# A two-layer encoder trunk on one core: VectorE takes branch B's finished block behind the split of the fourth chunk, where it stood in front of it

## The chip, the cores and the metric

The kernel runs on one core of a Trainium2 chip. The metric is the device time of one execution in microseconds. Three executions of the kernel before gave a median of 2657.65 us (2656.19 to 2660.18).

## The reference

The model is a trunk of two layers over 256 tokens with 2048 channels, all in float32.

```python
for l in range(DEPTH):                                  # 2
    h = rmsnorm(x, norm_mix[l])
    qa, ka, va, qi, ki, wi, qb, kb, vb = split(h @ w_in[l])
    o_a = dsa_branch(qa, ka, va, qi, ki, wi, bias_a)    # 8 heads x 128, top-64 keys
    o_b = swa_branch(qb, kb, vb, sinks[l], bias_b)      # 16 heads x 64, window of 128
    g_a, g_b = split(sigmoid(h @ w_gate[l]))
    merged = g_a * (o_a @ w_branch_a[l]) + g_b * (o_b @ w_branch_b[l])
    x = x + merged @ w_out[l]
    h = rmsnorm(x, norm_mlp[l])
    x = x + square(relu(h @ w_up[l])) @ w_down[l]
return rmsnorm(x, final_norm)
```

The change lies where `g_b * (o_b @ w_branch_b)` is finished and `merged` is formed.

## The kernel before, in words

**Chunks.** All weights stream from HBM once, in chunks of 256 rows by 512 columns (512 KB). A chunk takes four steps. SyncE issues its load into one of four `raw` buffers as soon as the chunk four places ahead of it has been split (`load_unit`, L336). ScalarE copies it, rounded, into `w_hi` (L934). VectorE forms the remainder `w_lo = raw - w_hi` (L1362). TensorE multiplies: for each of 2 row blocks and 2 token halves the three products hi·hi, hi·lo and lo·hi (L590 to L592), 12 matmuls of 512 columns. ScalarE may fill `w_hi` of a chunk once TensorE has finished the chunk four places before it, so the splits run up to four chunks ahead of TensorE.

**Wide chunks.** In some units the odd chunks 1, 3, 5 and 7 are wide: two by two blocks are multiplied with seven products where eight are usual (`seven_products`, L558 to L560, 21 matmuls of 256 columns). For these VectorE first forms sums of the chunk's blocks in `raw` (`weight_sums`, three subtractions and additions, L1371, L1375, L1377). ScalarE's copy has two pieces, the first (L941) straight from the load, the second (L943) from those sums, and VectorE's split covers seven quarters (`split_wide`, L1383). VectorE forms the sums of chunk c+1 before it splits chunk c.

**Branch B.** `C_MIXB` is the first chunk of branch B's part of a layer. For each of four column blocks n of 512 it has a gate unit of 8 chunks (four of them wide), `h @ w_gate`, and a branch unit of 4 plain chunks, `o_b @ w_branch_b`. Below, the chunks of block n are counted 0 to 7 (gate) and 8 to 11 (branch).

What happens with a block:
- When TensorE has finished the gate, ScalarE saves one quarter of the side products (`gate_side`, L1198). That stands in its order in the branch unit in front of chunk 11's copy.
- VectorE adds the side products together behind the split of chunk 11 (`add_up_sides`, L1781 to L1789).
- ScalarE applies tanh (`gate_tanh`, L1203) behind chunk 0's copy of the next gate unit. It is the sigmoid in disguise.
- VectorE takes the block in the next gate unit, at chunk 3 (`take_branch_b`, L1728). It waits for TensorE's end of the branch unit and for the tanh, multiplies gate and branch (L1732, twice), adds branch A's part (L1736), and transposes the sum in 32 by 32 blocks into `spread` (`spread_block`, L1440, twice).
- GpSimd stores `spread` to HBM (L465, 512 KB) and, when the store has landed, reads it back in another order into `moved` with four reads of 128 KB (L470, `pass_on`).
- ScalarE copies `moved`, rounded, into the operand of the output projection (`hi_moved`, L1001). In its order that stands behind chunk 8's copy, in front of chunks 9, 10, `gate_side` and 11. VectorE forms the remainder behind its split of chunk 8 (`lo_moved`, L1464).

The first gate unit of the part takes branch A's last block at the same place (`take_branch_a(3)`, L1720, two instructions, no transposes and no store). Branch B's last block is taken in the first unit of the output projection, whose chunks are all plain.

**Order.** Every engine's order is written out by hand. `unit` (L1386) walks the chunks of a unit: the sums for c+1, then `take` if c is 3, then `at[c]`, then the split of chunk c, then `then[c]`.

Of the kernel before, what the change touches and what calls it, by code (L numbers as in the profile page):

```python
# [114 lines left out]
def trunk_kernel(nc, x, w_misc, w_main, gains, sinks, rel_bias, onehot, final_gain, bias_rows, out):  # L115
    with ExitStack() as ctx:
# [1238 lines left out]
        def _(dve):  # L1355
# [30 lines left out]
            def unit(cl, chunks, take=None, turns=None, taken=None, jobs=None, width=NB, phase=0, first=0, sums=None,  # L1386
                     wide=(), steps=None, at=(), then=()):
                for c in range(first, chunks):
                    if c + 1 in wide:
                        weight_sums(cl, c + 1, steps(wide.index(c + 1)))  # L1390
                    if c == 3 and take:
                        take()
                    if c in at:
                        at[c]()
                    if c in wide:
                        split_wide(cl, c)
                    else:
                        split(cl, c, width, phase)
                    if c in then:
                        then[c]()  # L1400
                    if turns and c in (5, 7):
                        turns((c - 5) // 2)
                    if taken and c == 6:
                        taken()
                    if sums and c == 7:
                        sums()
                    if jobs:
                        jobs(c)

            def unit_done(cl_end):  # L1410
                dve.wait_ge(multiplied, cl_end + SLOTS)
# [24 lines left out]
            def spread_block(l, e, src, g=0):  # L1436

                spread_free(l, e, g)
                for t in range(TT):
                    last = nc.vector.transpose(spread[:, :, :, t, :].rearrange("p j k s -> p k j s"),  # L1440
                                               src[:, t, :].rearrange("p (k j s) -> p k j s", k=PIECES, j=QUARTERS))
                last.then_inc(spread_ready, 1)
# [18 lines left out]
            def lo_moved(l, e, hi, lo, g=0):  # L1461

                dve.wait_ge(moved_hi, g * NBLK + (l * TAKES + (e - E_M + 1)))
                nc.vector.tensor_tensor(pieces_of(lo), moved_pieces(), pieces_of(hi).bitcast(F32), ALU.subtract)\  # L1464
                    .then_inc(moved_took, 1)
# [232 lines left out]
            for l in range(DEPTH):  # L1698
# [10 lines left out]
                def take_stage(u):  # L1709
                    dve.wait_ge(act_took, l * ACT_UNITS + (u + 1))  # L1710
                    spread_block(l, E_QK + u if u < 6 else E_QB + u - 8, stage)

                for u in range(N_WIN):
                    take = take_keys if u == 0 else (lambda u=u: take_stage(u - 1)) if u <= 6 or u == 9 else None
                    unit(l * CHUNKS + (C_WIN + 8 * u), 8, take=take, jobs=lambda c, u=u: jobs_after(l, C_WIN + 8 * u + c - AHEAD))

                def cols(n):
                    return slice(n * NB, (n + 1) * NB)

                def take_branch_a(n):  # L1720
                    unit_done(l * CHUNKS + (C_MIXA + 12 * (n + 1)))
                    dve.wait_ge(act_took, l * ACT_UNITS + (10 + n + 1))
                    for t in range(TT):
                        last = nc.vector.scalar_tensor_tensor(out=mixed_a[:, t, cols(n)], in0=stage[:, t, :], scalar=1.0,
                                                              in1=acc[1][t][:], op0=ALU.add, op1=ALU.mult)
                    last.then_inc(dve_took, 1)

                def take_branch_b(n):  # L1728
                    unit_done(l * CHUNKS + (C_MIXB + 12 * (n + 1)))
                    dve.wait_ge(act_took, l * ACT_UNITS + (14 + n + 1))  # L1730
                    for t in range(TT):
                        last = nc.vector.scalar_tensor_tensor(out=stage2[:, t, :], in0=stage[:, t, :], scalar=1.0,  # L1732
                                                              in1=acc[1][t][:], op0=ALU.add, op1=ALU.mult)
                    last.then_inc(dve_took, 1)
                    dve.wait_ge(dve_took, l * DVE_UNITS + (4 + n + 1 + 1))
                    nc.vector.tensor_tensor(stage2[:], stage2[:], mixed_a[:, :, cols(n)], ALU.add).then_inc(mixed, 1)  # L1736
                    dve.wait_ge(mixed, l * NBLK + (n + 1))
                    spread_block(l, E_M + n, stage2)

                def gate_sums(n):  # L1740

                    hi, lo = (h_hl[:, part, PIECES * n + 2:PIECES * n + 4, :].rearrange("p k s -> p (k s)").bitcast(F32)
                              for part in range(2))
                    both = stage2[:, 1, :]
                    a11, a21, a12, a22 = (both[:, i * P:(i + 1) * P] for i in range(4))
                    s1, s2, s3, s4 = (sums_f[:, i * P:(i + 1) * P] for i in range(4))
                    chain.link(nc.vector.tensor_tensor(both, hi, lo, ALU.add))
                    nc.vector.tensor_tensor(s3, a21, a11, ALU.subtract)
                    chain.link(nc.vector.tensor_tensor(s1, a21, a22, ALU.add))
                    chain.link(nc.vector.tensor_tensor(s2, s1, a11, ALU.subtract))  # L1750
                    nc.vector.tensor_tensor(s4, a12, s2, ALU.subtract).then_inc(h_summed, 1)

                def gate_sums_lo(n):
                    dve.wait_ge(h_sums_hi, l * (G_SUMS + H_SUMS) + n + 1)
                    nc.vector.tensor_tensor(s_hh[:, 1, n, :], sums_f, s_hh[:, 0, n, :].bitcast(F32), ALU.subtract)\
                        .then_inc(h_sums_took, 1)

                def gate_sums_next(n):
                    gate_sums_lo(n)
                    gate_sums(n + 1)  # L1760

                for n in range(NBLK):
                    unit(l * CHUNKS + (C_MIXA + 12 * n), 8, phase=(C_MIXA + 12 * n) % RAW, take=(lambda n=n: take_branch_a(n - 1)) if n else (lambda: take_stage(9)),
                         jobs=lambda c, n=n: jobs_after(l, C_MIXA + 12 * n + c - AHEAD),
                         then={3: lambda: gate_sums(0), 5: lambda: gate_sums_next(0), 7: lambda: gate_sums_next(1)}
# [3 lines left out]
                         then={1: lambda: gate_sums_next(2), 3: lambda: gate_sums_lo(3)} if n == NBLK - 1 else ())  # L1769
# [4 lines left out]
                def add_up_sides(g, n, i):  # L1774

                    z, w = wide_acc[n // 2]
                    at = g * 2 + (l * LAYER_SIDES + i)
                    steps = g * 6 + 3 * (l * LAYER_SIDES + i)
                    quarters = stage[:].rearrange("p t (h c) -> p (t h) c", h=2)
                    dve.wait_ge(sides_out, at + 1)  # L1780
                    nc.vector.tensor_tensor(side_sum, z[:, 0:HALF], quarters[:, 1, :], ALU.add).then_inc(up_step, 1)  # L1781
                    dve.wait_ge(up_step, steps + 1)
                    nc.vector.tensor_tensor(quarters[:, 0::3, :], side_sum.unsqueeze(1).to_broadcast([P, 2, HALF]),
                                            w[:].rearrange("p (h c) -> p h c", h=2), ALU.subtract).then_inc(up_step, 1)
                    dve.wait_ge(up_step, steps + 2)
                    nc.vector.tensor_tensor(quarters[:, 2, :], quarters[:, 3, :], w[:, 0:HALF], ALU.subtract).then_inc(up_step, 1)
                    nc.vector.tensor_tensor(stage[:, 0, :], acc[0][0][:], stage[:, 0, :], ALU.add)
                    dve.wait_ge(up_step, steps + 3)
                    nc.vector.tensor_tensor(stage[:, 1, :], acc[0][1][:], stage[:, 1, :], ALU.add).then_inc(up_summed, 1)  # L1789

                def gate_steps(n):
                    return lambda i: 3 * (l * LAYER_WIDE + n * len(WIDE_GATE) + i)

                for n in range(NBLK):
                    unit(l * CHUNKS + (C_MIXB + 12 * n), 8,
                         take=(lambda n=n: take_branch_b(n - 1)) if n else (lambda: take_branch_a(3)),
                         wide=WIDE_GATE, steps=gate_steps(n))
                    then = {3: lambda n=n: add_up_sides(0, 0, n)}
                    if n:
                        then[0] = lambda n=n: lo_moved(l, E_M + n - 1, m_dst(n - 1, 0), m_dst(n - 1, 1))  # L1800
                    unit(l * CHUNKS + (C_MIXB + 12 * n + 8), 4, then=then)
# [45 lines left out]
                for n in range(NBLK):  # L1847
# [7 lines left out]
                    then = {7: lambda: lo_moved(l, E_M + 3, m_dst(3, 0), m_dst(3, 1))} if n == 0 else \  # L1855
# [115 lines left out]
                for n in range(1, NBLK):  # L1971
# [7 lines left out]
                    then = {3 if n > 1 else 5: x_add}  # L1979
# [124 lines left out]
```

## Time and profile before

| what | value |
|---|---|
| median of 3 executions | 2657.65 us (2656.19 to 2660.18) |
| profiled execution: time / span | 2660.85 us / 2659.0 us |
| TensorE's granted clock | 0.999 |
| busy share of the span: TensorE / weight load / VectorE / ScalarE / GpSimd | 100% / 83% / 78% / 55% / 9% |
| HBM read and written | 544.58 MB and 47.48 MB, 223 GB/s |

The span is from the first to the last instruction. The busy time of TensorE counts matmuls whose ends are modelled and that overlap, so a share of 100% says that TensorE is hardly ever without work, not that it is at its peak. Branch B's part of the first layer runs from 419 us to 548 us of the span, that of the second from 1736 us to 1867 us.

### The profile page before, as it was taken

The numbers are of one execution on the slowest core, as the hardware profiler recorded it, in microseconds if no ns is written. First come the engines' busy times: TensorE is split into PE (matmuls) and PEld (weight loads), VectorE is DVE, ScalarE is ACT, GpSimd is POOL, SyncE is SP. The second block draws the span as 40 slices with busy tenths as digits, with TensorE's granted clock in tenths as the row PEclk, the third lists the DMA queues.
The fourth block names the chain that finished last, engine by engine and source line by source line (L and its number), as shares of the span: only waits on it lengthen the run. The fifth ranks groups of instructions, "written<-read, shape, count | busy, mean of one in ns | idle before, by whom it ended". The sixth has DMA issues, their size and how long they took to land.

```text
span 2659.0 us, 37301 instructions
## 1 busy us (share of the span) xinstructions
PE 2646.0 (100%) x13432; PEld 2219.8 (83%) x13432; DVE 2080.4 (78%) x3099; ACT 1451.0 (55%) x1863; POOL 233.0 (9%) x408
## 2 busy tenths in 40 slices
PE   9999999999999999999999999999999999999998
PEld 7788778888888888888888887788888888888887
DVE  5677678977898997987756766789678989989875
ACT  5545555545565655645455455555456556556554
POOL 0103110000100100100010021100000001000000
PEclk9999999999999999999999999999999999999999
DMA  7887775776775766767677677667677767667574
GB/s 248 240 240 223 224 227 188 226 237 235 237 230 190 246 219 207 241 205 237 227 238 226 223 226 224 215 199 235 221 247 240 224 204 245 211 215 229 195 248 152
DMA packets 185092, 594.52 MB, mean 224 GB/s; under 512 B 25576, under 2 KB 43540, under 8 KB 184784
## 3 DMA queue, kind: packets, MB, share of 16 engines
q1 hardware_dynamic: 161936, 530.65, 61.2%
q0 software_dynamic: 22448, 61.16, 8.4%
q8 instruction: 106, 1.74, 0.3%
q14 instruction: 74, 0.61, 0.1%
q10 hardware_dynamic: 528, 0.37, 0.1%
HBM read 544.58 MB, written 47.48 MB: 223 GB/s over the span
## 4 chain that ended last, share of the span: by engine, by line
PE 96%; DVE 2%; DMA 1%; issue 0%; ACT 0%; SPq 0%; POOLq 0%; POOL 0%; ACTq 0%
PE acc L590 24%; PE acc L592 24%; PE acc L591 24%; PE att L558 2%; PE att L560 2%; PE att L559 2%; PE acc L558 2%; PE acc L560 2%; PE acc L559 2%; PE acc L608 1%; PE acc L607 1%; PE acc L606 1%; PE turn L559 1%; PE turn L560 1%; PE turn L558 1%; DMA raw<-in_w_main 0%
## 5 line engine op out<-in xcount | busy, mean ns | idle before, releaser
L1362 DVE TENSOR_TENSOR w_lo<-raw,w_hi 128x1024 fp32r<-128x1024 f32 (+1 forms) x778 | 933.5, 1211 | 372.0 <-ACT w_hi L934 367.8
L934 ACT ACTIVATE w_hi<-raw 128x1024 fp32r<-128x1024 f32 (+1 forms) x778 | 812.5, 1051 | 622.3 <-PE acc L592 437.8
L590 PE MATMUL acc<-w_hi,h_hl 128*128 128x512 f32 x1848 | 734.7, 398 | 1.1 <-DVE w_lo L1362 1.0
L592 PE MATMUL acc<-w_hi,h_hl 128*128 128x512 f32 x1848 | 729.0, 394 | 0.0
L591 PE MATMUL acc<-w_lo,h_hl 128*128 128x512 f32 x1848 | 728.7, 394 | 0.0
L590 PEld LDWEIGHTS acc<-w_hi,h_hl 128*128 128x128 f32 x1848 | 347.8, 188 | 83.6 <-issue 4.9
L592 PEld LDWEIGHTS acc<-w_hi,h_hl 128*128 128x128 f32 x1848 | 347.8, 188 | 81.6
L591 PEld LDWEIGHTS acc<-w_lo,h_hl 128*128 128x128 f32 x1848 | 348.2, 188 | 76.1
L590 PE MATMUL acc<-w_hi,o_hl 128*128 128x512 f32 x912 | 360.4, 395 | 0.0
L591 PE MATMUL acc<-w_lo,o_hl 128*128 128x512 f32 x912 | 360.0, 395 | 0.0
L592 PE MATMUL acc<-w_hi,o_hl 128*128 128x512 f32 x912 | 359.6, 394 | 0.0
L1383 DVE TENSOR_TENSOR w_lo<-raw,w_hi 128x1792 fp32r<-128x1792 f32 x166 | 335.6, 2022 | 30.0 <-ACT w_hi L943 29.1
L941 ACT ACTIVATE w_hi<-raw 128x768 fp32r<-128x768 f32 x166 | 140.4, 846 | 188.2 <-PE acc L560 102.4
L943 ACT ACTIVATE w_hi<-raw 128x1024 fp32r<-128x1024 f32 x166 | 175.2, 1056 | 98.1 <-DVE raw L1377 97.7
L592 PEld LDWEIGHTS acc<-w_hi,o_hl 128*128 128x128 f32 x912 | 171.7, 188 | 40.3
L590 PEld LDWEIGHTS acc<-w_hi,o_hl 128*128 128x128 f32 x912 | 171.6, 188 | 37.5 <-issue 1.1
L591 PEld LDWEIGHTS acc<-w_lo,o_hl 128*128 128x128 f32 x912 | 171.6, 188 | 36.4
L1371 DVE TENSOR_TENSOR raw<-raw 128x512 f32<-128x512 f32 x166 | 113.6, 684 | 26.6 <-DMA raw<-in_w_main 15.5
L465 POOL DMA_DIRECT2D scratch<-spread x36 | 20.3, 564 | 1207.0 <-DVE spread L1440 1207.0
L470 POOL DMA_DIRECT2D moved<-scratch x144 | 79.2, 555 | 122.1 <-DMA scratch<-spread 121.2
L1440 DVE STREAM_TRANSPOSE spread<-stage 128x512 f32<-128x512 f32 x112 | 73.0, 689 | 21.6 <-ACT stage L1140 17.5
L1032 ACT ACTIVATE probs<-probs,low 128x128 f32<-128x128 f32 x96 | 41.0, 428 | 67.8 <-DVE low L1547 35.0
(298 smaller groups left out, 3629.9 us busy)
## 6 DMA issues: line engine op xcount, KB each, us to landing
raw<-in_w_main SPq DMA_DIRECT2D x928, 512.0 KB, 4.3
scratch<-spread POOLq DMA_DIRECT2D x36, 512.0 KB, 3.3
moved<-scratch POOLq DMA_DIRECT2D x144, 128.0 KB, 5.0
scratch<-spread SPq DMA_DIRECT2D x31, 512.0 KB, 2.9
moved<-scratch SPq DMA_DIRECT2D x124, 128.0 KB, 3.2
scratch_p<-spread POOLq DMA_DIRECT2D x16, 384.0 KB, 4.5
moved<-scratch_p POOLq DMA_DIRECT2D x64, 96.0 KB, 4.3
raw<-in_w_misc SPq DMA_DIRECT2D x16, 336.0 KB, 4.0
```

The source lines that it names most:

```text
L558: nc.tensor.matmul(o, a_hi, hi[:, w], start=start, stop=False, skip_group_check=True)
L559: nc.tensor.matmul(o, a_hi, lo[:, w], start=False, stop=False, skip_group_check=True)
L560: return nc.tensor.matmul(o, a_lo, hi[:, w], start=False, stop=stop, skip_group_check=True)
L590: nc.tensor.matmul(o, a_hi, hi[:, kk], start=(k == 0), stop=False)
L591: nc.tensor.matmul(o, a_hi, lo[:, kk], start=False, stop=False)
L592: last = nc.tensor.matmul(o, a_lo, hi[:, kk], start=False, stop=fin)
L934: nc.scalar.activation(w_hi[s][:, 0:2 * width], raw[r][:, 0:2 * width], ACT.Copy).then_inc(hi_ready, 1)
L941: nc.scalar.activation(w_hi[s][:, 0:3 * HALF], raw[s][:, HALF:CW], ACT.Copy)
L943: nc.scalar.activation(w_hi[s][:, 3 * HALF:7 * HALF], raw[s][:, CW:2 * CW], ACT.Copy).then_inc(hi_ready, 1)
L1362: nc.vector.tensor_tensor(w_lo[s][:, 0:2 * width], raw[r][:, 0:2 * width], w_hi[s][:, 0:2 * width].bitcast(F32), ALU.subtract).then_inc(lo ...
L1371: nc.vector.tensor_tensor(r[:, 4 * HALF:6 * HALF].rearrange("p (k n) -> p k n", k=2), r[:, HALF:3 * HALF].rearrange("p (k n) -> p k n", k= ...
L1383: nc.vector.tensor_tensor(w_lo[s][:, 0:7 * HALF], raw[s][:, HALF:8 * HALF], w_hi[s][:, 0:7 * HALF].bitcast(F32), ALU.subtract).then_inc(lo ...
```

## The change

`take_branch_b(n - 1)`, and in the first gate unit `take_branch_a(3)`, goes from `take`, which runs in front of the split of chunk 3, to `then[3]`, which runs behind it.

```diff
                 for n in range(NBLK):
                     unit(l * CHUNKS + (C_MIXB + 12 * n), 8,
-                         take=(lambda n=n: take_branch_b(n - 1)) if n else (lambda: take_branch_a(3)),
+                         then={3: (lambda n=n: take_branch_b(n - 1)) if n else (lambda: take_branch_a(3))},
                          wide=WIDE_GATE, steps=gate_steps(n))
```

The orders of TensorE, ScalarE, GpSimd and SyncE stay as they are. VectorE's differs in eight places, four in each layer.

VectorE in the gate units of blocks 1, 2 and 3: L1362 is the split of chunk 2, L1383 that of the wide chunk 3, L1732 to L1440 the taking of block n - 1, and L1371 and L1375 the sums of chunk 5.

```order
 L1377 TENSOR_TENSOR raw<-raw 128x256
 L1362 TENSOR_TENSOR w_lo<-raw,w_hi 128x1024
+L1383 TENSOR_TENSOR w_lo<-raw,w_hi 128x1792
 L1732 SCALAR_TENSOR_TENSOR stage<-stage,acc 128x512 x2
 L1736 TENSOR_TENSOR stage<-stage,qk 128x1024
 L1440 STREAM_TRANSPOSE spread<-stage 128x4x4x32 x2
-L1383 TENSOR_TENSOR w_lo<-raw,w_hi 128x1792
 L1371 TENSOR_TENSOR raw<-raw 128x512
 L1375 TENSOR_TENSOR raw<-raw 128x256
```

The split of chunk 3 moved up past five instructions; the sums of chunk 5 follow both as before.

VectorE in the gate unit of block 0, where L1724 is the taking of branch A's last block:

```order
 L1377 TENSOR_TENSOR raw<-raw 128x256
 L1362 TENSOR_TENSOR w_lo<-raw,w_hi 128x1024
+L1383 TENSOR_TENSOR w_lo<-raw,w_hi 128x1792
 L1724 SCALAR_TENSOR_TENSOR qk<-stage,acc 128x512 x2
-L1383 TENSOR_TENSOR w_lo<-raw,w_hi 128x1792
 L1371 TENSOR_TENSOR raw<-raw 128x512
 L1375 TENSOR_TENSOR raw<-raw 128x256
```

Here the split moved up past two instructions.

## Rows read from the trace of the kernel before

**Rows 1.** Chain of work that ended last, shares of the span by engine.

```profile
PE 96%; DVE 2%; DMA 1%; issue 0%; ACT 0%; SPq 0%; POOLq 0%; POOL 0%; ACTq 0%
```

**Rows 2.** TensorE's waits: line, for whom; us in total, times, longest.

```profile
PE acc L590 <- DVE w_lo L1362: 1.0, 1, 1.0
```

**Rows 3.** Timeline of VectorE, gate unit 1, layer 0: start, length (us), engine, line, operation.

```profile
448.41 2.03 DVE L1383 TENSOR_TENSOR w_lo<-raw,w_hi 128x1792 fp32r<-128x1792 f32 x1 [0.43 <-ACT w_hi L943]
450.35 0.69 DVE L1371 TENSOR_TENSOR raw<-raw 128x512 f32<-128x512 f32 x1
...
451.88 1.22 DVE L1362 TENSOR_TENSOR w_lo<-raw,w_hi 128x1024 fp32r<-128x1024 f32 x1
453.01 1.28 DVE L1732 SCALAR_TENSOR_TENSOR stage<-stage,acc 128x512 f32<-128x512 f32 x2
...
455.59 1.31 DVE L1440 STREAM_TRANSPOSE spread<-stage 128x512 f32<-128x512 f32 x2
456.81 1.98 DVE L1383 TENSOR_TENSOR w_lo<-raw,w_hi 128x1792 fp32r<-128x1792 f32 x1
458.72 0.68 DVE L1371 TENSOR_TENSOR raw<-raw 128x512 f32<-128x512 f32 x1
...
460.24 1.22 DVE L1362 TENSOR_TENSOR w_lo<-raw,w_hi 128x1024 fp32r<-128x1024 f32 x1
...
473.70 1.23 DVE L1362 TENSOR_TENSOR w_lo<-raw,w_hi 128x1024 fp32r<-128x1024 f32 x1 [0.86 <-ACT w_hi L934]
```

**Rows 4.** Timeline of TensorE, first matmuls of chunk 4: gate units 0 and 1.

```profile
429.30 0.39 PE L590 MATMUL acc<-w_hi,h_hl 128*128 128x512 f32 x1
429.53 0.39 PE L591 MATMUL acc<-w_lo,h_hl 128*128 128x512 f32 x1
...
461.53 0.48 PE L590 MATMUL acc<-w_hi,h_hl 128*128 128x512 f32 x1
461.85 0.39 PE L591 MATMUL acc<-w_lo,h_hl 128*128 128x512 f32 x1
```

**Rows 5.** Timeline of ScalarE, gate and branch unit 1, layer 0.

```profile
451.99 1.07 ACT L943 ACTIVATE w_hi<-raw 128x1024 fp32r<-128x1024 f32 x1
...
468.08 1.04 ACT L1001 ACTIVATE o_hl<-moved 128x1024 fp32r<-128x1024 f32 x1
469.05 1.06 ACT L934 ACTIVATE w_hi<-raw 128x1024 fp32r<-128x1024 f32 x1
...
472.33 0.39 ACT L1198 ACTIVATE stage<-att 128x256 f32<-128x256 f32 x1 [1.01 <-PE acc L560]
```

**Rows 6.** Timeline of GpSimd, the store and four reads of units 1 and 2.

```profile
457.19 0.56 POOL L465 DMA_DIRECT2D scratch<-spread  x1 [66.77 <-DVE spread L1440]
460.36 2.19 POOL L470 DMA_DIRECT2D moved<-scratch  x4 [2.61 <-DMA scratch<-spread]
...
492.76 2.33 POOL L470 DMA_DIRECT2D moved<-scratch  x4 [2.70 <-DMA scratch<-spread]
```

**Rows 7.** L470 alone, unit 1, layer 0 (460 to 463 us): issue to landing.

```profile
DMA to landing us min/median/max: 3.1/4.7/6.0
```

**Rows 8.** L470 alone, unit 2, layer 0 (492 to 495.3 us): issue to landing.

```profile
DMA to landing us min/median/max: 3.3/5.2/6.7
```

**Rows 9.** Timeline of ScalarE, branch unit 2, layer 0.

```profile
501.28 1.06 ACT L1001 ACTIVATE o_hl<-moved 128x1024 fp32r<-128x1024 f32 x1
...
504.69 0.39 ACT L1198 ACTIVATE stage<-att 128x256 f32<-128x256 f32 x1
```

**Rows 10.** Timeline of VectorE: gate unit 0, first output unit, gate unit 1 of layer 1.

```profile
424.54 1.22 DVE L1362 TENSOR_TENSOR w_lo<-raw,w_hi 128x1024 fp32r<-128x1024 f32 x1
...
548.15 1.28 DVE L1732 SCALAR_TENSOR_TENSOR stage<-stage,acc 128x512 f32<-128x512 f32 x2 [0.40 <-PE acc L592]
...
1782.28 0.69 DVE L1371 TENSOR_TENSOR raw<-raw 128x512 f32<-128x512 f32 x1 [1.78 <-DMA raw<-in_w_main]
```

**Rows 11.** L470 over the whole span, 144 reads: issue to landing.

```profile
DMA to landing us min/median/max: 2.8/5.0/7.7
```

## The prediction

> **What bounds the kernel now.** I read the chain of work that ended last first: TensorE holds 96% of it [rows 1]. So a saving counts only where TensorE stands still, and a loss only where it makes TensorE stand still. The list of TensorE's waits has a single entry inside a gate unit: 1.0 us, once, for a low half from VectorE [rows 2]. That is all there is to gain, apart from delays too short for the list.
>
> One of those short ones decides this case, so I read the timelines of gate unit 1 next. At chunk 4 TensorE's second matmul starts 0.32 us after the first (461.85 against 461.53), where 0.23 is the pace at the same place in gate unit 0 (429.53 against 429.30) [rows 4]. VectorE ended chunk 4's split at 460.24 + 1.22 = 461.46 [rows 3]. The 0.09 us is TensorE held by VectorE. Hence **at chunk 4 of gate units 1 to 3 the slack is nil**: whatever makes VectorE later there makes the kernel longer by as much. In gate unit 0 the same split ended at 424.54 + 1.22 = 425.76, 3.5 us before TensorE began the chunk [rows 4, 10].
>
> VectorE's work up to that point is one chain: from ScalarE's `gate_side` at 472.33 through chunk 11's copy and split (VectorE idles 0.86 us for it [rows 3, 5]), the adding of sides, tanh, the splits of chunks 0 to 3, the taking, and so to chunk 4. Its idle spots are waits for ScalarE inside this chain. So a late `gate_side` passes on in full.
>
> **The change, part by part.** Nothing is added or removed.
>
> *The wide split of chunk 3 goes ahead of the taking.* Before, the taking runs from 453.01 to 456.81, 3.80 us, and the split follows at 456.81 [rows 3]. ScalarE's high half of chunk 3 is there at 451.99 + 1.07 = 453.06 [rows 5], and VectorE leaves chunk 2's split at 453.10 [rows 3]. So the split can start at about 453.09 and loses next to nothing. Chunk 3 is then ready 3.7 us earlier. TensorE hardly waits for chunk 3, because chunk 4 holds it a moment later; value nil.
>
> *Chunk 4.* The same two pieces of work stand ahead of the sums of chunk 5 and the split of chunk 4, in another order. A wide split takes 450.35 - 448.41 = 1.94 us from start to start [rows 3]. New start of the sums: 453.09 + 1.94 + 3.80 = 458.83, against 458.72 [rows 3]: 0.1 us later, and there is no slack. Price 0.1 us in a gate unit that is otherwise on time. From below, 0 if the split need not wait for the high half.
>
> *Chunk 7's load* waits for chunk 3's split, so it is issued 3.7 us earlier. In gate unit 1 of layer 1 VectorE idled 1.78 us for that load [rows 10], and this is the place of the 1.0 us that TensorE waited [rows 2]. It goes. Value -1.0 us in the profiled execution, and 0 in one that had no such collision.
>
> *The taking itself is 2.0 us later* (453.01 to 455.03), and its store and four reads with it, on GpSimd's queue; nothing else is queued behind them there. Who waits? TensorE needs the freed bank only at chunk 8, far off. The next in line is `hi_moved` on ScalarE, and behind it in ScalarE's order stand chunks 9 and 10 and `gate_side`, the head of VectorE's chain.
>
> In unit 1 the reads start to be issued at 460.36, the last of four 1.64 us later (three quarters of 2.19) [rows 6]. It lands 6.0 us after that [rows 7], at 468.0, and `hi_moved` starts at 468.08 [rows 5]: they meet almost exactly, so the cover is already used up on this side. What is left is ScalarE's idle time before `gate_side`. Three steps at 0.97 us (469.05 - 468.08) lead from `hi_moved` to `gate_side`, which could have started at 471.0 and did at 472.33. With the landing 2.02 us later, `hi_moved` starts at 470.1 and `gate_side` at 473.0: **0.7 us late**, paid at chunk 4 of gate unit 2.
>
> In unit 2 the last read is issued at 492.76 + 1.75 = 494.5 [rows 6] and lands 6.7 us on [rows 8], at 501.2; `hi_moved` starts at 501.28, `gate_side` at 504.69 [rows 9]. Here only 0.5 us is spare. 501.2 + 2.02 + 0.08 + 2.9 = 506.2: **1.5 us late**, paid at chunk 4 of gate unit 3. The store and the reads of that unit shift with TensorE, so the two prices add.
>
> In unit 3 the same delay falls on the first output unit, where VectorE itself waits 0.40 us for TensorE at the taking [rows 10] and no chunk is wide: nil. Gate unit 0 takes a short block without a store and has 3.5 us of slack: nil.
>
> **A rule against the trace.** The whole price hangs on the reads. Rows first: the last of four lands 6.0 and 6.7 us after its own issue [rows 7, 8], with weight loads in flight beside it. The Trainium skill, "DMA: Bandwidth & Descriptors", section "Anatomy of one DMA — SWDGE (gpsimd) path", gives about 2.0 us plus the bytes over 436 GB/s, an estimate of 2.3 us for 128 KB. By it the moved block would be there at about 466, before `hi_moved`'s turn, and the delay would be nil. The trace disagrees by a factor of over two, so the sum goes by the rows.
>
> **Sum.** A layer: 0.1 (gate unit 1) + 0.7 + 1.5 = 2.3 us. I take layer 1 at the price of layer 0, since its passes are the same. Two layers 4.6, less 1.0 for the late load and 0.1 for the short stalls that the new ones contain: **+3.5 us**. The profiled execution took 2660.85 us (span 2659.0), 3.2 above the median; +3.5 on it is 2664.3. On the median of 2657.65 it is 2661.1 us, +0.13%. What a measurement of this kernel can tell from no change is about 0.2%, 5.3 us.
>
> **Rivals.**
>
> *Covered.* With chunk 7's load out of the way early, the reads meet fewer packets, or wait behind chunk 8's load and no more, and land 2 us sooner relative to the store. For it: the first of the four lands in 3.1 us [rows 7], so the rest is queueing. Against: the loads of chunks 8 and 9 now lie on the reads as those of 7 and 8 did. Then only chunk 4's price stays, 0.1 in each of six gate units, less 1.0 and 0.1: -0.5 us, 2657.1. The rule above would bring this case about.
>
> *Slower, by the same path.* The reads of the whole run last up to 7.7 us [rows 11]. If the shifted reads meet two loads in each of the four places, the last lands in unit 1 at 460.36 + 1.64 + 2.02 + 7.7 = 471.7, so `gate_side` starts at 474.7, 2.4 us late. Four times that, plus 0.2 and less 1.1, is +8.7 us: 2666.4. It decides from 1.55 us a place on, that is when the last read takes over 6.9 us.
>
> *The split gains nothing and waits.* The high half was ready only 0.04 us before VectorE. Were ScalarE late, VectorE would stand idle at the split and chunk 4 would be late by that. ScalarE's copy hangs on TensorE's end of chunk 11, which is early when VectorE is late, so the two exclude each other; I give it no price beyond the 0.1.
>
> *Faster by over 0.2%.* TensorE's waits in these units come to about 1.6 us in all (1.0 and six times 0.1), so 5.3 us is not there to be had.
>
> **How the numbers follow.** Forecast (+1.5 to +5.3): 0.52. Covered: 0.25. Slower: 0.20. Faster for a reason that the trace doesn't show: 0.03. The forecast's upper end spills about 0.05 over the bound. So faster 0.03, within 0.2% 0.72, slower 0.25. The range takes in the covered case with the scatter of the runs (1.5 us below the median), and most of the slower one: 2656.0 to 2666.0. The likeliest case alone is 2659.0 to 2663.0.
>
> **What would show it.** Right, if in the new trace chunk 3's split starts at the high half's end and the taking directly behind it; if ScalarE shows waits for DMA in front of `hi_moved` (L1001) in branch units 1 and 2; if `gate_side` (L1198) then starts without idle time before it; and if TensorE's waits at chunk 4 of gate units 2 and 3 grow to 0.7 and 1.5 us. The late load at gate unit 1 of layer 1 must be gone. Wrong, if `hi_moved` doesn't wait, or if it waits and TensorE doesn't.

## The result, and the profile after

| | before | changed |
|---|---|---|
| median of 8 executions each | 2657.64 us (2656.19 to 2660.99) | 2666.42 us (2664.72 to 2669.32) |
| ratio, with its 95% interval | | 1.0031 [1.0022, 1.0040] |
| profiled execution: time / span | 2660.85 / 2659.0 us | 2669.05 / 2667.3 us |
| granted clock of TensorE | 0.999 | 0.999 |

The changed kernel is 8.8 us slower, 0.3%, and the interval lies wholly above no change. The forecast was 3.5 us slower, 2661.1 us in a range of 2656.0 to 2666.0; the measured median lies 0.4 us above that range.

The page's chain of work that ended last, by engine (it answers to [rows 1]):

```profile
PE 84%; DVE 7%; DMA 4%; issue 2%; ACT 1%; POOL 0%; SPq 0%; DVEq 0%; POOLq 0%; ACTq 0%
```

TensorE's share fell from 96% to 84%, and VectorE and DMA took its place. The share says which way the chain runs and is no measure of the loss: 12% of the span would be 320 us. Every engine has as many instructions as before, and none is busy for more than 1.2 us longer. The waits of TensorE in branch B's part of layer 0 and of layer 1, each as line, for whom, total, times, longest (they answer to [rows 2], where the only entry was 1.0 us in layer 1):

```profile
PE acc L590 <- DVE w_lo L1362: 3.5, 3, 1.7
...
PE acc L590 <- DVE w_lo L1362: 3.3, 2, 1.7
```

They make 6.8 us. The late load of [rows 10] and its 1.0 us are gone, so 5.8 us of the spans' difference of 8.3 shows as waits here. Delays too short for the list come out when the same matmul is looked up in both traces. Where gate unit 1 of layer 0 begins, the changed kernel is 0.34 us late already (451.31 against 450.97). At the end of layer 0's part it is 4.62 us late (552.81 against 548.19), where layer 1's part begins 6.85 (1743.01 against 1736.16), and at its end 8.85 (1876.01 against 1867.16). So 4.3 + 2.0 = 6.3 us of the 8.3 arise in branch B's part. Another 2.2 us arise between the two parts, 0.9 us of them as two listed waits in the first layer's MLP, where the profile before has none. Two kernels below that lose nothing on the median fall behind in the same stretch, by 0.9 us (reads from SyncE) and 1.1 us (half reads), so that this is the change's doing isn't shown.

TensorE's timeline at chunk 4 of gate units 2 and 3 and at chunk 9 of unit 3 in layer 0, then at chunk 4 of gate units 2 and 3 in layer 1:

```profile
496.18 0.50 PE L590 MATMUL acc<-w_hi,h_hl 128*128 128x512 f32 x1 [1.71 <-DVE w_lo L1362]
...
530.14 0.50 PE L590 MATMUL acc<-w_hi,h_hl 128*128 128x512 f32 x1 [1.43 <-DVE w_lo L1362]
...
544.11 0.50 PE L590 MATMUL acc<-w_hi,o_hl 128*128 128x512 f32 x1 [0.36 <-DVE w_lo L1362]
...
1819.61 0.51 PE L590 MATMUL acc<-w_hi,h_hl 128*128 128x512 f32 x1 [1.69 <-DVE w_lo L1362]
...
1853.69 0.50 PE L590 MATMUL acc<-w_hi,h_hl 128*128 128x512 f32 x1 [1.58 <-DVE w_lo L1362]
```

The place is the one that was named: chunk 4 of the gate unit after the late store, in VectorE's chain behind `gate_side`. VectorE's timeline at the moved place, gate unit 1 of layer 0 (it answers to [rows 3]):

```profile
452.22 1.22 DVE L1362 TENSOR_TENSOR w_lo<-raw,w_hi 128x1024 fp32r<-128x1024 f32 x1
453.43 2.03 DVE L1383 TENSOR_TENSOR w_lo<-raw,w_hi 128x1792 fp32r<-128x1792 f32 x1
455.37 1.28 DVE L1732 SCALAR_TENSOR_TENSOR stage<-stage,acc 128x512 f32<-128x512 f32 x2
...
459.18 0.65 DVE L1371 TENSOR_TENSOR raw<-raw 128x512 f32<-128x512 f32 x1
```

The split starts without a wait and the taking directly behind it. From the split of chunk 2 to the sums of chunk 5 it is 459.18 - 452.22 = 6.96 us, where it was 458.72 - 451.88 = 6.84: the order itself costs 0.1 us, as was worked out. ScalarE's timeline of the same unit (it answers to [rows 5]):

```profile
466.42 1.04 ACT L934 ACTIVATE w_hi<-raw 128x1024 fp32r<-128x1024 f32 x1
471.48 1.06 ACT L1001 ACTIVATE o_hl<-moved 128x1024 fp32r<-128x1024 f32 x1 [4.02 <-DMA moved<-scratch]
472.44 1.99 ACT L934 ACTIVATE w_hi<-raw 128x1024 fp32r<-128x1024 f32 x2
474.34 0.36 ACT L1198 ACTIVATE stage<-att 128x256 f32<-128x256 f32 x1
474.60 2.10 ACT L934 ACTIVATE w_hi<-raw 128x1024 fp32r<-128x1024 f32 x2
```

ScalarE stands still for 4.02 us in front of `hi_moved` (L1001), then runs chunks 9 and 10 and `gate_side` (L1198) back to back. `gate_side` no longer waits for TensorE. It starts at 474.34, where [rows 5] has 472.33; less the 0.34 us by which the whole unit is late, that is 1.7 us, and TensorE's wait at chunk 4 of gate unit 2 is 1.71. Over the whole run, the idle time in front of L1001 (us, times) before and changed:

```profile
  DMA moved<-scratch: 1.8, 2
...
  DMA moved<-scratch: 29.1, 10
```

The last read is what `hi_moved` waits for. Issue to landing of the four reads (L470) in units 1 and 2 of layer 0, which answers to [rows 7, 8]:

```profile
DMA to landing us min/median/max: 4.0/5.5/7.1
...
DMA to landing us min/median/max: 4.6/5.9/6.7
```

In unit 1 the last read took 7.1 us where it had taken 6.0; in unit 2 it stayed at 6.7. The same of units 1 and 2 in layer 1, before in the first fence and changed in the second:

```profile
DMA to landing us min/median/max: 3.0/5.7/7.5
...
DMA to landing us min/median/max: 2.9/4.4/5.3
```

```profile
DMA to landing us min/median/max: 4.0/5.8/7.0
...
DMA to landing us min/median/max: 3.5/5.4/6.8
```

Here the last read went from 7.5 to 7.0 us and from 5.3 to 6.8 us.

### The profile page after: what moved, and what is told of

The parts are those of the page before. It is cut to its first block, busy times and chain, and to the rows that moved or that the text cites. A ratio compares the mean times of both kernels' runs of the same rounds, so it can differ in the third digit from the quotient of the medians.

```text
span 2667.3 us, 37301 instructions
## 1 busy us (share of the span) xinstructions
PE 2647.2 (99%) x13432; PEld 2218.9 (83%) x13432; DVE 2079.2 (78%) x3099; ACT 1446.7 (54%) x1863; POOL 232.2 (9%) x408
## 3 DMA queue, kind: packets, MB, share of 16 engines
q8 instruction: 106, 1.74, 0.3%
## 4 chain that ended last, share of the span: by engine, by line
PE 84%; DVE 7%; DMA 4%; issue 2%; ACT 1%; POOL 0%; SPq 0%; DVEq 0%; POOLq 0%; ACTq 0%
PE acc L590 22%; PE acc L592 21%; PE acc L591 21%; DVE w_lo L1362 2%; PE att L558 2%; PE att L560 2%; PE att L559 2%; PE acc L558 2%; PE acc L560 2%; PE acc L559 2%; DMA moved<-scratch 2%; PE acc L606 1%; PE acc L608 1%; PE acc L607 1%; DVE w_lo L1383 1%
## 5 line engine op out<-in xcount | busy, mean ns | idle before, releaser
L1362 DVE TENSOR_TENSOR w_lo<-raw,w_hi 128x1024 fp32r<-128x1024 f32 (+1 forms) x778 | 932.0, 1211 | 369.5 <-ACT w_hi L934 365.2
L1383 DVE TENSOR_TENSOR w_lo<-raw,w_hi 128x1792 fp32r<-128x1792 f32 x166 | 335.8, 2023 | 27.2 <-ACT w_hi L943 26.5
L1371 DVE TENSOR_TENSOR raw<-raw 128x512 f32<-128x512 f32 x166 | 113.3, 682 | 27.4 <-DMA raw<-in_w_main 16.9
L470 POOL DMA_DIRECT2D moved<-scratch x144 | 79.0, 553 | 120.3 <-DMA scratch<-spread 119.4
L1440 DVE STREAM_TRANSPOSE spread<-stage 128x512 f32<-128x512 f32 x112 | 73.0, 690 | 19.1 <-ACT stage L1140 14.9
```

Of the source, the lines that this page charges most:

```text
L1362: nc.vector.tensor_tensor(w_lo[s][:, 0:2 * width], raw[r][:, 0:2 * width], w_hi[s][:, 0:2 * width].bitcast(F32), ALU.subtract).then_inc(lo ...
L1371: nc.vector.tensor_tensor(r[:, 4 * HALF:6 * HALF].rearrange("p (k n) -> p k n", k=2), r[:, HALF:3 * HALF].rearrange("p (k n) -> p k n", k= ...
L1383: nc.vector.tensor_tensor(w_lo[s][:, 0:7 * HALF], raw[s][:, HALF:8 * HALF], w_hi[s][:, 0:7 * HALF].bitcast(F32), ALU.subtract).then_inc(lo ...
```

## The experiments

Theory A: the later store and reads hold `hi_moved` and, behind it in ScalarE's order, `gate_side`. Rival B: VectorE's new order itself delays chunk 4. Rival C: the shifted transfers hurt the weight loads. Each kernel was timed in five rounds against the kernel before on its chip; its median there was 2659.28 us for the first four runs, 2658.26 for the next four and 2658.89 for the last two.

### ScalarE's copy behind chunk 10

```diff
 # on the changed kernel; branch unit, ScalarE
-then={0: lambda n=n: hi_moved(l, E_M + n - 1, m_dst(n - 1, 0))} if n else ())
+then={2: lambda n=n: hi_moved(l, E_M + n - 1, m_dst(n - 1, 0))} if n else ())
 # branch unit, VectorE
-then[0] = lambda n=n: lo_moved(...)
+then[2] = lambda n=n: lo_moved(...)
```

> The changed kernel, with ScalarE's copy of the moved block (L1001) and VectorE's remainder (L1464) put behind chunk 10 of the branch unit, where they stood behind chunk 8. Theory A (the loss is the later store and reads, which hold ScalarE's copy and so gate_side, L1198): the copy now stands one step in front of gate_side instead of three; with the reads landing as in the changed kernel it starts near 471.5 and gate_side near 472.5, on time within 0.2 us. Time -1 to +2 us against the kernel before (2657 to 2660), waits of TensorE at chunk 4 of gate units 2 and 3 at most 0.4 us. Rival B (VectorE's new order itself delays chunk 4): the loss stays, +6 to +9 us. Rival C (the shifted transfers hurt the weight loads): the loss stays above +4 us, with waits for DMA in front of splits.

Measured: 2666.51 us (2662.46 to 2670.62), ratio 1.0029 [1.0018, 1.0041]. The loss stayed, against the expectation of theory A. ScalarE's timeline of unit 1 of this kernel shows why (all of it stands 2.05 us earlier in the span than in the kernel before):

```profile
464.02 1.05 ACT L934 ACTIVATE w_hi<-raw 128x1024 fp32r<-128x1024 f32 x1
468.18 1.06 ACT L934 ACTIVATE w_hi<-raw 128x1024 fp32r<-128x1024 f32 x1 [3.12 <-DMA raw<-in_w_main]
469.69 1.06 ACT L934 ACTIVATE w_hi<-raw 128x1024 fp32r<-128x1024 f32 x1 [0.45 <-DMA raw<-in_w_main]
470.66 1.04 ACT L1001 ACTIVATE o_hl<-moved 128x1024 fp32r<-128x1024 f32 x1
471.61 0.37 ACT L1198 ACTIVATE stage<-att 128x256 f32<-128x256 f32 x1
```

With the copy out of the way, chunk 9 itself is late: ScalarE waits 3.12 us for its load, then 0.45 us for chunk 10's. Chunk 9's load is the one issued among the reads. It took 6.6 us here:

```profile
DMA to landing us min/median/max: 6.6/6.6/6.6
```

So the copy of the moved block is one of two things that hold `gate_side`, and the weight loads are the other. Theory A in its narrow form failed, and a loss that stays, with waits for weight loads, is what rival C had said for this run. What follows I call theory D; it is A and C together: a weight load that is issued while the reads run lands only about when the last of them does. Before, that was chunk 8's: it was issued at 461.5 and took 5.6 us, while the last read landed at 468.0. In the changed kernel it is chunk 9's, issued at 463.9, 7.2 us, beside a last read at 464.4 + 7.1 = 471.5. In all six places of the changed kernel chunk 9's load landed 0.3 to 0.5 us ahead of the last read. Chunk 8's load, issued 0.8 us ahead of the first read, took 3.2 us in unit 1. The two kernels' single loads, before (chunk 8, chunk 9) in the first fence and changed (chunk 8, chunk 9) in the second:

```profile
DMA to landing us min/median/max: 5.6/5.6/5.6
...
DMA to landing us min/median/max: 5.5/5.5/5.5
```

```profile
DMA to landing us min/median/max: 3.2/3.2/3.2
...
DMA to landing us min/median/max: 7.2/7.2/7.2
```

### The same later place on the kernel before

The same two lines, on the kernel before.

> The kernel before with the same later place for the copy and the remainder, the taking still in front of the split. Theory A: the copy was barely on time before, so little changes: -1.5 to +0.5 us. Rivals B and C say nothing else here; it is the control for the first run.

Measured: 2660.31 us (2657.61 to 2662.53), ratio 1.0007 [0.9998, 1.0016]. No loss that can be told from none.

### The store alone held back

```diff
 # on the kernel before; GpSimd
 for n in range(MIXED_MOVES):
+    pool.wait_ge(spread_ready, l * MOVES + E_M + n + 1)
+    pool.wait_ge(lo_ready, l * CHUNKS + (C_MIXB + 12 * (n + 1)) + RAW + 4)
     pass_on(l, E_M + n)
```

> The kernel before, VectorE's order unchanged; GpSimd alone waits in front of its store of blocks 0 to 2 until VectorE has split chunk 3, so the store leaves about 1.6 us later (near 458.8 in gate unit 1) and nothing else moves. Theory A: most of the loss comes back, some 0.4 us less in each of four places than in the changed kernel, and the late load stays: +4 to +8 us. Rival B: no loss, within 1 us of the kernel before.

Measured: 2671.70 us (2670.13 to 2672.79), ratio 1.0049 [1.0035, 1.0062], +12.4 us. VectorE's order is that of before, so a later store alone is enough to make a loss, without rival B. It is larger than the +4 to +8 us expected: chunk 7's load is issued by the same split and meets the store, and the reads wait 4.15 us for the store to land, where they had waited 2.61 [rows 6]. In unit 1 of layer 1 they wait 7.02 us. VectorE's transposes of unit 1, then GpSimd's timeline of unit 1 and its reads in unit 1 of layer 1 (L1442 is L1440 here, and L1385 the wide split L1383, as the edit adds two lines):

```profile
453.44 1.30 DVE L1442 STREAM_TRANSPOSE spread<-stage 128x512 f32<-128x512 f32 x2
...
457.20 0.56 POOL L465 DMA_DIRECT2D scratch<-spread  x1 [69.76 <-DVE w_lo L1385]
461.91 2.18 POOL L470 DMA_DIRECT2D moved<-scratch  x4 [4.15 <-DMA scratch<-spread]
...
1787.54 2.18 POOL L470 DMA_DIRECT2D moved<-scratch  x4 [7.02 <-DMA scratch<-spread]
```

The store's start, 457.20, looks like that of [rows 6], but in this execution the unit stands 2.15 us earlier in the span (transposes at 453.44, before at 455.59 [rows 3]), so the store is 2.2 us late. In the changed kernel chunk 7's load, issued at 455.5, lands 3.9 us later, just ahead of the store at 459.55, and the reads there wait 2.62 us for the store. This part of the loss is spared.

### The change in two gate units at a time

```diff
-take=(lambda n=n: take_branch_b(n - 1)) if n else (lambda: take_branch_a(3)),
+take=(lambda n=n: take_branch_b(n - 1) if n else take_branch_a(3)) if n not in (1, 2) else None,
+then={3: (lambda n=n: take_branch_b(n - 1) if n else take_branch_a(3))} if n in (1, 2) else (),
```

> The change in gate units 1 and 2 alone; units 0 and 3 as before. Theory A: a late store in unit n is paid at chunk 4 of gate unit n+1, and unit 3's is followed by a unit without wide chunks, so units 1 and 2 hold nearly all of the loss: +7 to +9 us. Rival B (paid where the split stands): two of three gate units that take a block, +5 to +6 us, with a wait at chunk 4 of gate unit 1 as large as at unit 2.

Measured with units 1 and 2: 2664.82 us (2663.14 to 2666.94), ratio 1.0022 [1.0012, 1.0031], +5.5 us, below theory A's span and inside B's. At chunk 4 of gate unit 1, though, where B wants its wait, there is none in TensorE's timeline; the matmul starts 0.34 us before the next, about as in [rows 4]:

```profile
461.42 0.50 PE L590 MATMUL acc<-w_hi,h_hl 128*128 128x512 f32 x1
461.76 0.39 PE L591 MATMUL acc<-w_lo,h_hl 128*128 128x512 f32 x1
```

The waits of layer 0 stand at chunk 4 of gate unit 2 (1.74 us) and, as unit 3 keeps the old order, at chunk 3 of gate unit 3 (1.38 us).

> The change in gate units 0 and 3 alone, units 1 and 2 as before. Theory A (a late store is paid at chunk 4 of the next gate unit): unit 3 has no gate unit behind it and unit 0 no store, so the time is that of the kernel before within -0.5 to +2 us (up to 0.6 us a layer may be paid at a branch chunk of unit 3 itself). Rival B (the order itself): a third of the loss or more, +3 us and over.

Measured with units 0 and 3 (`(0, 3)` for `(1, 2)`): 2658.13 us (2657.13 to 2661.88), ratio 1.0000 [0.9991, 1.0009]. Half of the places cost nothing. The loss hangs on units 1 and 2, whose block is followed by another gate unit. The two halves add to 5.5 us and not to 8.8. Matmul beside matmul with the kernel before, units 1 and 2 alone lose 5.3 us in branch B's parts and 0.2 us between them, the changed kernel 6.3 and 2.2. The first difference fits unit 3: its taking is itself late when unit 2's is, and its own 0.36 us at chunk 9 appears only then. The second stays open.

This run leaves units 1 and 2 as they were, and so shows how far the reads' length scatters without being moved. Issue to landing of L470 in units 1 and 2 of layer 0:

```profile
DMA to landing us min/median/max: 3.6/5.2/6.5
...
DMA to landing us min/median/max: 3.2/5.2/7.0
```

In the kernel before the last of them took 6.0 and 6.7 us there [rows 7, 8]. Nor does this run have the late load of [rows 10], though gate unit 1 of layer 1 is as before: that collision isn't there in every execution.

### Shorter reads

```diff
 # GpSimd, in branch B alone: runs = 1 (a quarter) or 2 (half)
-pool.dma_start(dst[32 * jj:32 * jj + 32],
-    bass.AP(scratch, jj * size, [[NB * TT, 32], [32 * NB * TT, QUARTERS], [1, size]]))
+pool.dma_start(dst[32 * jj:32 * jj + 32, 0:runs],
+    bass.AP(scratch, jj * size, [[NB * TT, 32], [32 * NB * TT, runs], [1, size]]))
```

> The changed kernel with the four reads of blocks 0 to 2 in branch B cut to a quarter of their bytes (only the first of four runs of each partition is read; three quarters of those operands are left as they were, so that part of the result is not computed). Theory A and theory D (D: not ScalarE's copy alone, but every weight load issued while the reads run lands only with the last of them; that is chunk 9's now and was chunk 8's before): the last read and chunk 9's load land 2 to 4 us earlier, gate_side is on time, and the loss goes: -2 to +1.5 us against the kernel before. Rival B: the loss stays, +6 us or more.

Measured with a quarter on the changed kernel: 2659.11 us (2656.15 to 2659.91), ratio 1.0000 [0.9991, 1.0009].

> The kernel before with the same short reads (the same part is not computed): the control. Theories A and D: its reads were just in time, so -2 to +0.5 us; the pair of this run and the changed kernel with short reads then differ by less than 1.5 us, where the full reads differ by 8.8.

Measured on the kernel before: 2658.66 us (2656.93 to 2661.32), ratio 1.0003 [0.9994, 1.0012]. The two orders of VectorE now take the same time.

> The changed kernel with GpSimd's four reads of blocks 0 to 2 in branch B cut to half of their bytes (half of those operands is left as it was, so that part of the result is not computed). Theories A and D: the last read lands about midway between 5.7 us (a quarter) and 8.7 us (all) from the first issue, near 7.2, where the copy has 6.9 before it is late: -1 to +2.5 us. If the loss hung on something else of the reads, say their number or their place, it would stay above +4 us.

Measured with half: 2658.63 us (2657.71 to 2662.17), ratio 1.0000 [0.9991, 1.0009]. Issue to landing of L470 in unit 1, a quarter, then half:

```profile
DMA to landing us min/median/max: 2.8/3.0/4.4
```

```profile
DMA to landing us min/median/max: 2.8/4.0/5.3
```

**The whole loss goes when the reads are shortened**, and half of their bytes is enough. In the kernel with a quarter, `gate_side` waits for TensorE again, and ScalarE's wait for chunk 10's load is 0.42 us:

```profile
466.19 1.06 ACT L1001 ACTIVATE o_hl<-moved 128x1024 fp32r<-128x1024 f32 x1 [1.17 <-DMA moved<-scratch]
467.15 1.04 ACT L934 ACTIVATE w_hi<-raw 128x1024 fp32r<-128x1024 f32 x1
468.62 1.06 ACT L934 ACTIVATE w_hi<-raw 128x1024 fp32r<-128x1024 f32 x1 [0.42 <-DMA raw<-in_w_main]
470.31 0.39 ACT L1198 ACTIVATE stage<-att 128x256 f32<-128x256 f32 x1 [0.63 <-PE acc L560]
```

### Store and reads issued by SyncE

```diff
-MIXED_MOVES = E_XO - 1 - E_M
+MIXED_MOVES = 0
 # SyncE, gate units of branch B; late=True on the changed kernel (both behind chunk 7's load)
-load_unit(l, C_MIXB + 12 * n, 8)
+load_unit(l, C_MIXB + 12 * n, 8, pass_on(l, E_M + n - 1) if n else None, late=False)
```

> The kernel before with store and reads of blocks 0 to 2 in branch B issued by SyncE (store in front of chunk 7's load, reads behind it), where GpSimd issued them. Theories A and D: if SyncE's reads land in 3 to 4 us from their issue, as its others do in the trace before (median 3.2), the block is there some 2 us sooner and no late load is left in layer 1: -2.5 to +0.5 us. If they queue like GpSimd's, or the reads hold up chunk 8's load on the same queue: +1 to +4 us. Rival B says nothing.

Measured on the kernel before: 2659.12 us (2657.38 to 2661.14), ratio 1.0001 [0.9992, 1.0010].

> The changed kernel, complete, with store and reads of blocks 0 to 2 in branch B issued by SyncE behind chunk 7's load, where GpSimd issued them. In the run of the kernel before with SyncE's reads the last read landed 8.7 us after the store's issue, where GpSimd's took 10.8; with the store at 459.3 in gate unit 1 that is 468.0, where the kernel before had it. Theories A and D: gate_side is on time again, loss nearly gone, -1 to +2.5 us. Rival B (VectorE's order): +6 us or more.

Measured on the changed kernel: 2659.24 us (2657.32 to 2662.00), ratio 1.0000 [0.9991, 1.0009]. This kernel computes everything, has VectorE's new order and GpSimd's old transfers on another queue, and the loss is gone from the median. In its profile two of TensorE's waits are left at chunk 4 of gate units 2 and 3 in layer 0, of 0.22 and 0.76 us. Issue to landing of its reads (L358) in unit 1, and ScalarE's timeline there:

```profile
DMA to landing us min/median/max: 2.6/2.9/3.4
```

```profile
468.43 1.06 ACT L934 ACTIVATE w_hi<-raw 128x1024 fp32r<-128x1024 f32 x1 [2.30 <-DMA raw<-in_w_main]
469.40 1.05 ACT L1001 ACTIVATE o_hl<-moved 128x1024 fp32r<-128x1024 f32 x1
470.35 2.00 ACT L934 ACTIVATE w_hi<-raw 128x1024 fp32r<-128x1024 f32 x2
472.38 0.38 ACT L1198 ACTIVATE stage<-att 128x256 f32<-128x256 f32 x1
```

The last read now lands by 462.8 + 3.4 = 466.2, and `hi_moved` has no wait. `gate_side` starts at 472.38, as in [rows 5] (472.33). The queue is not all that changed, though. SyncE's timeline of issues:

```profile
455.10 0.33 SPq L336 DMA_DIRECT2D raw<-in_w_main  x1
458.90 0.33 SPq L352 DMA_DIRECT2D scratch<-spread  x1
461.50 1.75 SPq L358 DMA_DIRECT2D moved<-scratch  x4
463.29 0.92 SPq L336 DMA_DIRECT2D raw<-in_w_main  x2
```

In SyncE's order the loads of chunks 8 and 9 stand behind the reads (463.29), where chunk 8's left at 461.9 in the changed kernel, and chunk 7's landed 3.6 us after 455.10, ahead of the store. So the reads are issued with no weight load in flight. In the run before this one, with chunk 7's load in flight beside them, SyncE's reads took 3.4 to 4.8 us in unit 1. How much is the queue's and how much the order's, these two runs don't tell. No version was faster than the kernel before beyond its interval.

## Why the prediction was right or wrong

- **What bounds the kernel, and where the slack is nil**: right. All the new waits of note stand at chunk 4 of gate units 2 and 3, for the low half from VectorE.
- **The order itself, 0.1 us**: right, 6.96 against 6.84 us. With short reads both orders take the same time within their intervals.
- **The late load goes**: the wait at gate unit 1 of layer 1 is gone, but the run with units 0 and 3, where that unit is as before, has none there either. The 1.0 us belonged to the profiled execution, as the prediction allowed; its sum took it off the median all the same.
- **The store 2 us later is paid through `hi_moved` and `gate_side`**: right in place and in kind, and shown by the runs that shorten the reads or issue them from SyncE. It was incomplete: the run with the copy moved shows chunk 9's load as a second hold, equally late.
- **The size**: here the forecast was too small. The terms were 0.7 us at gate unit 2 and 1.5 at gate unit 3, 4.4 in two layers. Measured were 1.71 and 1.43 in layer 0, 1.69 and 1.58 in layer 1, 6.4 in all. The step that failed is "with the landing 2.02 us later, `hi_moved` starts at 470.1", with layer 1 taken at layer 0's price: I shifted the landing by the store's delay and kept the reads' lengths of one layer in one execution, 6.0 and 6.7 us. The last reads took 7.1, 6.7, 7.0 and 6.8 us, together 2.2 us more than the sum had, and the waits are 2.0 us more. In unit 1 of layer 0 `hi_moved` started at 471.48; 0.34 of the 1.38 us beyond 470.1 is the lateness of the whole unit, the rest the longer read. In unit 2 of layer 0, where the length stayed, the term came out right. That the move itself makes the reads longer isn't shown: unmoved, the last read took 5.3 to 7.5 us in the four places of the kernel before, and 6.5 and 7.0 in layer 0 of the run with units 0 and 3.
- **Unit 3 nil**: wrong by 0.36 us in layer 0, at chunk 9, which the copy had made late.
- **Rivals**: the measured +8.8 us is the one that ended slower, at +8.7 and with the same path. Its condition, a last read over 6.9 us after its issue, is about met (7.1, 6.7, 7.0 and 6.8 us), but its price of 2.4 us a place was not: four places at 1.4 to 1.7 make 6.4, and the rest of the median's difference lies in unit 3, in small delays and between the two parts. That the sum fits better than its terms is luck. It had 0.20, too little: the row with 7.7 us over the whole run spoke for it, and so did the 7.5 us in unit 1 of layer 1. The covered case, and with it the Trainium skill's fixed cost and rate ("DMA: Bandwidth & Descriptors", section "Anatomy of one DMA — SWDGE (gpsimd) path"), did not come about for GpSimd's full reads, at 7.1 us where its estimate was 2.3.

The runs leave three things open: how much of each wait is the copy's and how much chunk 9's load's, since every cure shortened both; whether it is SyncE's queue or its order that shortens the reads; and where the 2.2 us between the two parts of the profiled execution come from.

## What to carry to other kernels

An engine's order can be neutral for that engine and still cost time, as here, because a store or load that it triggers moves against all the other transfers: follow the moved step to its last landing, and ask which load it then overlaps. Do not carry a transfer's length over from one reading: the last of the same four reads took 5.3 to 7.5 us in four like places of one execution. Read all like places, and give the longest of them a price and a fair chance. Where a cover has already run out on one side (a consumer that starts 0.1 us after its data lands), a delay passes on, less the idle time that is left further down (1.3 us in front of `gate_side` in unit 1).

## What the hardware showed that I had not expected

- The same four reads of 128 KB landed 4.0 to 7.1 us after their issue from GpSimd in unit 1 of the changed kernel, and 2.6 to 3.4 us from SyncE (up to 5.0 us over the three units of layer 0). In the first case weight loads were in flight before and among them, in the second none was in flight, in unit 1, until the last read had been issued. Behind SyncE's reads it was chunk 8's load that waited: ScalarE stood 2.30 us for it, and the median lost nothing.
- A weight load issued while GpSimd's reads ran took 5.6 us (before) and 7.2 us (changed), where one issued 2 us earlier in the changed kernel took 3.2 us. In all six places of the changed kernel the load issued among the reads landed 0.3 to 0.5 us ahead of the last read.
- Holding a store back by its semaphore alone made the kernel 12.4 us slower, more than the change that moved the work with it. In one place the store then took 7.3 us to land.
